# Loading the seventh chunk of modulation weights earlier, and starting VectorE's multiply-and-sums behind the second chunk, in the first stage of a hybrid attention / mLSTM / conv layer on one core

## The chip, the core and the metric

The kernel runs on one core of a Trainium2 chip (trn2). Its engines are TensorE (PE, with its weight load PEld), VectorE (DVE), ScalarE (ACT), GpSimd (POOL) and SyncE (SP, which only issues transfers). The metric is the device time of one execution in microseconds; lower is better.

## The reference

One inference step of a one-layer diffusion backbone over 128 context tokens and 512 latent tokens of width 1024. What the first stage computes is the modulated, normalised input and its first projections:

```
mod = (silu(cond) @ w_ada + b_ada).reshape(B, 6, D)       # cond: c for latent, c_ctx for context tokens
shift1, scale1, gate1, shift2, scale2, gate2 = mod[:, 0..5, None, :]
h = rmsnorm(x, g_pre_mix) * (1 + scale1) + shift1
(na_q, na_k, na_v, m_q, ..., gate_pre) = split(h @ w_in)
```

Everything is float32. The rest of the layer (neighbourhood attention, a bidirectional mLSTM, a short convolution, three gated branches, an output projection, and a SwiGLU feed-forward block) takes the tokens from `h` on.

## The kernel before

All 640 tokens (T) are held at once. The model dimension is cut into eight chunks of 128 (KD = 8). Every large product is made from three float32r matmuls: each operand is split into a high part (a copy to `fp32r` on ACT: `w_hi`, `h_hi`) and a low part (a subtraction on DVE: `w_lo`, `h_lo`), and PE multiplies high by high, high by low and low by high (L2070, L2071, L2072).

A Python function `make_plan` writes one list of steps, and each engine walks the same list and does its part of each step. So the order of the list is the order on every engine, and an engine that waits in one step holds everything behind it. Semaphores are counted.

The first stage runs like this. The tokens are loaded, normalised and turned (steps `xsq`, `xturn`), which gives `xnt`, chunk by chunk, with the channel on the partition. For each chunk k the stage then needs `scale1` and `shift1` of its 128 channels for the two conditions, in `mod`. For chunks 0 to 5 PE makes them: `rows(k)` is an `ada_row` group (16 small matmuls of the chunk's weights `ada0[:, k]` with `cond`, L2117, copied to `adarow` by ACT, L1202), `columns(k)` is an `ada_pair` group (4 matmuls, L2125; DVE adds the bias and the norm weight, L1584 and L1588). For chunks 6 and 7 (`DOT_CHUNKS`) DVE makes them: step `dot k m` is two multiply-and-sums over a row of 1024 (L1744), one for each condition, of half m of `ada0[:, k]` with `condr0`; after the half m = 1 come two small instructions (L1752, L1755). `condr0` holds the two condition rows, the same on all 128 partitions, after a SiLU on ACT (step `dots_in`, L1321). The products themselves go to `prod0s`, which is laid over the token tile `xt`, as is `condr0`.

Step `h k` applies scale and shift to `xnt[:, k]` (DVE for k up to 3, L1766; ACT above, L1332), step `hsplit k` makes `h_hi` (ACT, L1338) and `h_lo` (DVE, L1773), and step `first k` is the part of the first projection (the attention values of all tokens, accumulated in five PSUM banks, 15 matmuls per chunk) that chunk k gives. Called below: unit k. `split_to(n)` makes the high and low part of weight blocks up to n (L1102 and L1476). Block b of weights lies in `raw[:, b % 4]`.

In the list before, `dots_in` stands behind unit 0. `dot 6 0` stands behind `hsplit 3`, `dot 6 1` between `h 4` and `hsplit 4`, `dot 7 0` between `h 5` and `hsplit 5`, and `dot 7 1` between `h 6` and `hsplit 6`.

All loads of the stage but one are issued by SP, in this order: the token tiles and small constants, then `ada0` for chunks 0 to 7, with block 0, 1, 2, 3 of the weights behind chunk 0, 2, 4 and 6, then the other constants, `wm`, the key cache, and the weight blocks from 4 on as their buffers come free. The transfers of one issuing engine are worked off as a queue on the 16 DMA engines. The one exception is `condr0`: GpSimd issues it, when the last token tile is turned (`x_tr`), because it overwrites `xt`.

Of the kernel before, what the change touches and what calls it, by code (L numbers as in the profile page):

```python
# [19 lines left out]
ACT = mybir.ActivationFunctionType  # L20
X = mybir.AxisListType.X

P = 128
D = 1024
KD = D // P
CTX, LAT = 128, 512
T = LAT + CTX
HT = T // 2
TT = T // P
# [77 lines left out]
BLOCKS_HELD = 4  # L107
FIRST_ADA = 8
DOT_CHUNKS = (6, 7)


def parts_of(n):
# [58 lines left out]
def make_plan():  # L171
# [3 lines left out]
    plan, groups = [], []  # L175
# [103 lines left out]
    plan.append(("hsplit", 0))  # L279
    rows(1)  # L280
    columns(1)
    plan += [("h", 1), ("hsplit", 1)]
    dots = [(k, m) for k in DOT_CHUNKS for m in range(2)]
    for k in range(KD):
        c = k + 2
        plan.append(("first", k, 0, 2))
        if c < DOT_CHUNKS[0]:
            rows(c)
        plan.append(("first", k, 2, TT))
        if c < DOT_CHUNKS[0]:  # L290
            columns(c)
        if k % 2 == 0 and c < KD:
            split_to(k // 2 + 2)
        if k == 0:
            plan.append(("dots_in",))
        if c < KD:
            plan.append(("h", c))
            if k in (2, 3, 4):
                plan.append(("dot", *dots.pop(0)))
            plan.append(("hsplit", c))  # L300
            if k == 1:
                plan.append(("dot", *dots.pop(0)))
        if k == 5:
            split_to(5)
        if k == 6:
            group("mif", mif, 0, 0, bank=4)
            group("mif", mif, 0, 1, bank=5)
            split_to(6)
# [76 lines left out]
    m = UNIT_OF[("out", (1,))]  # L385
# [66 lines left out]
    for c in range(2):  # L452
        for i in range(6):
            m = UNIT_OF[("down", (c, i))]
# [114 lines left out]
def program(nc, a, out, vline, gline, xline):  # L569

    ctx = ExitStack()
    with ctx:
# [3 lines left out]
        def at(name, shape, offset, dt=F32):  # L576

            size = 4
            for n in shape[1:]:
                size *= n  # L580
            assert offset + size <= ROOM, name
            return nc.alloc_sbuf_tensor_at(name, shape, dt, offset=base + offset)
# [40 lines left out]
        xnt = at("xnt", [P, KD, T], R1 + 20480)  # L623
        junk = at("junk", [P, D], R1 + 40960 + 2048)
        ada0 = at("ada0", [P, FIRST_ADA, KD * UW], ROOM - FIRST_ADA * KD * UW * 4)
        condr0 = at("condr0", [P, 2, D], R1)
        prod0s = [at(f"dot{c}", [P, D], R1 + 8192 + 4096 * c) for c in range(2)]

        (bo_hi, bo_lo, cl, cout, hsum, mnat, mcols, dec, e_sb, st_sb, kw_sb, tmp_sb, num_sb, merged, gt), _e = chain(
# [42 lines left out]
        def sems(names):  # L672
# [14 lines left out]
        condr0_in, condr0_rd, dot_done, dot_bias, dot_mod = sems(  # L687
            "condr0_in condr0_rd dot_done dot_bias dot_mod")
# [12 lines left out]
        x_sq, x_rstd, x_nrm, x_tr = sems("x_sq x_rstd x_nrm x_tr")  # L701
# [130 lines left out]
        def _(sp):  # L832
            sp.dma_start(cols[:, :], a["cols"]).then_inc(cols_in, 16)
            def load(b):
                if D0 <= b < D0 + BLOCKS_HELD:
                    sp.wait_ge(flo_done, 7 * (WU - 2 + (b - D0) // 2) + 7)
                elif b >= BLOCKS_HELD and is_ada(b - BLOCKS_HELD):
                    sp.wait_ge(ada_done, adas_done(b - BLOCKS_HELD))
                elif b >= BLOCKS_HELD:
                    wait_lo(sp, b - BLOCKS_HELD)  # L840
                sp.dma_start(raw[:, b % BLOCKS_HELD, :], source(b)).then_inc(raw_in[b % BLOCKS_HELD], 16)
# [14 lines left out]
            for t in range(TT):  # L856
                src = a["x_sample"][0, tok(t), :] if t < CH else a["x_prompt"][0]
                sp.dma_start(xt[:, t, :], src).then_inc(x_in[t], 16)
                if t == 0:
                    sp.dma_start(cst[:, 0:160], a["consts"][:, 0:160]).then_inc(const_in, 16)  # L860
            for j in range(KD):
                sp.dma_start(ada0[:, j, :], a["w_first"][j]).then_inc(ada_in[j], 16)
                if j % 2 == 0:
                    load(j // 2)
            sp.dma_start(cst[:, 160:640], a["consts"][:, 160:640]).then_inc(const2_in, 16)
            sp.dma_start(wm[:, :, :], a["w_mif"]).then_inc(wm_in, 16)
            sp.dma_start(kct[:, :, :], a["cache_k"]).then_inc(kc_in, 16)
            for step in PLAN:
# [44 lines left out]
                elif step[0] == "ada_rows":  # L913
# [9 lines left out]
                    src = bass.AP(gline.tensor, q * 2 * D, [[0, P], [D, 2], [1, D]])  # L923
# [39 lines left out]
        def _(pool):  # L963
# [20 lines left out]
            def bias(hp):  # L984
# [6 lines left out]
                for y, free in ((0, 1), (1, 3), (2, 4)):  # L991
# [6 lines left out]
                            braw[:, i, :].rearrange("p (r k) -> p r k", r=ROWS)[:, :, sh:sh + KB],  # L998
                            mask_na[:, y, :].unsqueeze(1).to_broadcast([P, ROWS, KB]), ALU.add)
                    ins.then_inc(bias_rd, 1)  # L1000

            pool.wait_ge(x_tr, 2 * TT)
            src = bass.AP(a["cond_rows"].tensor, 0, [[0, P], [D, 2], [1, D]])
            pool.dma_start(condr0[:, :, :], src).then_inc(condr0_in, 16)
            pool.wait_ge(const2_in, 16)
            for step in PLAN:
                if step[0] == "bias0":
# [40 lines left out]
                elif step[0] == "group" and GROUPS[step[1]]["kind"] == "mo":  # L1048
                    x = GROUPS[step[1]]
                    f, h = x["what"]  # L1050
# [32 lines left out]
        def _(act):  # L1083
# [207 lines left out]
            for step in PLAN:  # L1291
# [26 lines left out]
                    drain(step[1])  # L1318
                elif step[0] == "dots_in":
                    act.wait_ge(condr0_in, 16)  # L1320
                    nc.scalar.activation(condr0[:, :, :], condr0[:, :, :], ACT.Silu).then_inc(condr0_rd, 1)  # L1321
                elif step[0] == "h" and step[1] > 3:
                    k = step[1]
                    act.wait_ge(xt_dve, TT)
# [10 lines left out]
                elif step[0] == "hsplit":  # L1335
                    k = step[1]
                    act.wait_ge(h_aff, k + 1)
                    nc.scalar.activation(h_hi[:, k, :], xnt[:, k, :], ACT.Copy).then_inc(h_hid, 1)  # L1338
                elif step[0] == "na":
                    _, sub, s = step  # L1340
# [122 lines left out]
        def _(dve):  # L1463
# [240 lines left out]
            for step in PLAN:  # L1704
# [30 lines left out]
                elif step[0] == "dot":  # L1735

                    k, m = step[1:]
                    dve.wait_ge(condr0_rd, 1)
                    dve.wait_ge(ada_in[k], 16)
                    n = 2 * DOT_CHUNKS.index(k) + m  # L1740
                    if n:
# [27 lines left out]
                elif step[0] == "hsplit":  # L1769

                    k = step[1]
                    dve.wait_ge(h_hid, k + 1)
                    nc.vector.tensor_tensor(h_lo[:, k, :], xnt[:, k, :], h_hi[:, k, :].bitcast(F32),  # L1773
                                            ALU.subtract).then_inc(h_lod, 1)
                elif step[0] == "na":
# [724 lines left out]
```

## Time and profile before

| | |
|---|---|
| median of 3 runs | 1149.83 us (1148.89 to 1150.03) |
| the profiled execution's own time | 1150.59 us |
| its span | 1148.8 us |
| TensorE busy | 1128.4 us, 98% of the span |
| VectorE busy | 725.4 us, 63% |
| ScalarE busy | 477.5 us, 42% |
| GpSimd busy | 71.2 us, 6% |
| mean granted TensorE clock | 0.997 |

The span runs from the first to the last instruction record of the profiled execution; its own time has 1.8 us more around it. All times below are microseconds from the start of the span. A row of the timeline gives start, duration, engine, line, operation, output and input, and in brackets how long the engine was idle before and what released it. Durations of back-to-back matmuls overlap; the pace is the distance of their starts.

### The profile page before, as it was taken

The numbers are of one execution on the slowest core, as the hardware profiler recorded it, in microseconds if no ns is written. First come the engines' busy times: TensorE is split into PE (matmuls) and PEld (weight loads), VectorE is DVE, ScalarE is ACT, GpSimd is POOL, SyncE is SP. The second block draws the span as 40 slices with busy tenths as digits, with TensorE's granted clock in tenths as the row PEclk, the third lists the DMA queues.
The fourth block names the chain that finished last, engine by engine and source line by source line (L and its number), as shares of the span: only waits on it lengthen the run. The fifth ranks groups of instructions, "written<-read, shape, count | busy, mean of one in ns | idle before, by whom it ended". The sixth has DMA issues, their size and how long they took to land.

```text
span 1148.8 us, 18558 instructions
## 1 busy us (share of the span) xinstructions
PE 1128.4 (98%) x7358; PEld 1061.3 (92%) x7358; DVE 725.4 (63%) x1290; ACT 477.5 (42%) x881; POOL 71.2 (6%) x123
## 2 busy tenths in 40 slices
PE   5999999999999999999999999999999999999997
PEld 4699999889999999999999988999999999988886
DVE  4724545449675666588795446899997777633444
ACT  4544443443334334322222337655555555533431
POOL 2032111000000000220000002100000000000002
PEclk9999999999999999999999999999999999999999
DMA  9666121132431121336654244234322232315112
GB/s 364 231 194 146 56 75 56 37 92 74 76 73 55 56 74 56 111 128 185 202 177 136 68 137 155 81 130 146 129 83 102 75 119 103 110 56 196 61 37 92
DMA packets 40150, 130.22 MB, mean 113 GB/s; under 512 B 8736, under 2 KB 10304, under 8 KB 38528
## 3 DMA queue, kind: packets, MB, share of 16 engines
q1 hardware_dynamic: 36592, 121.41, 32.6%
q0 software_dynamic: 3472, 7.62, 2.3%
q8 instruction: 59, 0.97, 0.4%
q14 instruction: 27, 0.22, 0.1%
HBM read 121.64 MB, written 7.36 MB: 112 GB/s over the span
## 4 chain that ended last, share of the span: by engine, by line
PE 92%; DVE 5%; ACT 1%; issue 1%; DMA 1%; SPq 0%; POOL 0%; POOLq 0%; ACTq 0%; DVEq 0%
PE ps L2070 28%; PE ps L2072 28%; PE ps L2071 28%; PE ps L2275 1%; PE ps L2314 1%; PE ps L2298 1%; PE ps L2366 1%; PE ps L2368 1%; PE ps L2370 1%; DMA xt<-in_x_sample 1%; PE ps L2242 1%; PE ps L2352 0%; PE ps L2117 0%; DVE w_lo L1476 0%; DVE dot L1744 0%
## 5 line engine op out<-in xcount | busy, mean ns | idle before, releaser
L2072 PE MATMUL ps<-h_hi,w_lo 128*128 128x320 f32 x1184 | 365.9, 309 | 0.0
L2070 PE MATMUL ps<-h_hi,w_hi 128*128 128x320 f32 x1024 | 322.6, 315 | 0.2 <-DVE w_hi L1601 0.2
L2071 PE MATMUL ps<-h_lo,w_hi 128*128 128x320 f32 x1024 | 316.3, 309 | 0.0
L2072 PEld LDWEIGHTS ps<-h_hi,w_lo 128*128 128x128 f32 x1184 | 222.3, 188 | 0.0
L1476 DVE TENSOR_TENSOR w_lo<-raw,w_hi 128x1024 fp32r<-128x1024 f32 x109 | 132.7, 1227 | 111.7 <-ACT w_hi L1102 111.2
L2070 PEld LDWEIGHTS ps<-h_hi,w_hi 128*128 128x128 f32 x1024 | 192.6, 188 | 2.4 <-DVE w_hi L1601 0.5
L2071 PEld LDWEIGHTS ps<-h_lo,w_hi 128*128 128x128 f32 x1024 | 192.5, 188 | 0.1
L2070 PE MATMUL ps<-w_hi,h_hi 128*128 128x512 f32 x380 | 151.0, 397 | 1.2 <-DVE h_lo L1773 1.1
L2072 PE MATMUL ps<-w_hi,h_lo 128*128 128x512 f32 x380 | 148.6, 391 | 0.0
L2071 PE MATMUL ps<-w_lo,h_hi 128*128 128x512 f32 x380 | 148.4, 391 | 0.0
L1102 ACT ACTIVATE w_hi<-raw 128x1024 fp32r<-128x1024 f32 x109 | 113.3, 1052 | 32.9 <-PE ps L2072 32.3
L2070 PEld LDWEIGHTS ps<-w_hi,h_hi 128*128 128x128 f32 x380 | 71.6, 188 | 18.8 <-issue 4.0
L2072 PEld LDWEIGHTS ps<-w_hi,h_lo 128*128 128x128 f32 x380 | 71.6, 188 | 15.3
L2071 PEld LDWEIGHTS ps<-w_lo,h_hi 128*128 128x128 f32 x380 | 71.7, 189 | 14.1
L1193 ACT ACTIVATE gt<-ps,half_bg 128x320 f32<-128x320 f32 x48 | 25.4, 529 | 137.7 <-PE ps L2072 137.7
L2070 PE MATMUL ps<-h_hi,w_lo 128*128 128x320 f32 x240 | 74.4, 310 | 0.8 <-ACT snap L1240 0.8
L2071 PE MATMUL ps<-h_lo,w_lo 128*128 128x320 f32 x240 | 74.2, 309 | 0.0
L2070 PE MATMUL ps<-tt_hi,w_hi 128*128 128x320 f32 x240 | 73.9, 308 | 0.0
L2071 PE MATMUL ps<-tt_lo,w_hi 128*128 128x320 f32 x240 | 73.9, 308 | 0.0
L2072 PE MATMUL ps<-tt_hi,w_hi 128*128 128x320 f32 x240 | 73.9, 308 | 0.0
L1522 DVE TENSOR_TENSOR h_lo<-ff,h_hi 128x1280 fp32r<-128x1280 f32 (+1 forms) x22 | 30.5, 1429 | 64.4 <-ACT h_hi L1130 64.4
L1489 DVE SCALAR_TENSOR_TENSOR prod<-raw,condr 128x1024 f32<-128x1024 f32 x48 | 57.1, 1227 | 14.1 <-ACT condr L1314 12.9
(275 smaller groups left out, 1836.3 us busy)
## 6 DMA issues: line engine op xcount, KB each, us to landing
raw<-in_w_blocks SPq DMA_DIRECT2D x182, 512.0 KB, 3.8
ada<-in_w_first SPq DMA_DIRECT2D x8, 1024.0 KB, 19.4
xline<-x SPq DMA_DIRECT2D x5, 512.0 KB, 5.3
x<-xline SPq DMA_DIRECT2D x5, 512.0 KB, 8.0
xt<-in_x_sample SPq DMA_DIRECT2D x4, 512.0 KB, 6.7
condr<-in_cond_rows POOLq DMA_DIRECT2D x2, 1024.0 KB, 7.0
vtok<-vline POOLq DMA_DIRECT2D x8, 256.0 KB, 10.4
g<-gline SPq DMA_DIRECT2D x2, 1024.0 KB, 6.9
```

What stands on the lines that cost most here:

```text
L1102: ins = nc.scalar.activation(held(w_hi, b), raw[:, s, :], ACT.Copy)
L1193: nc.scalar.activation(gt[:, f, half(h)], bank, ACT.Tanh, scale=0.5, bias=half_bg[:, t:t + 1]).then_inc(act_drain, 1)
L1476: nc.vector.tensor_tensor(held(w_lo, b), raw[:, s, :], held(w_hi, b).bitcast(F32), ALU.subtract).then_inc(lo_done, 1)
L1489: ins = nc.vector.scalar_tensor_tensor(prod[c][:, :], raw[:, b % BLOCKS_HELD, :], 1.0, condr[:, c, :], ALU.mult, ALU.mult, accum_out=to)
L1522: nc.vector.tensor_tensor(h_lo[:, o2 + k:o2 + k + n, :], ff[:, k0 + k:k0 + k + n, :], h_hi[:, o2 + k:o2 + k + n, :].bitcast(F32), ALU.subt ...
L2070: nc.tensor.matmul(dst, wh, xh, start=first, stop=False, skip_group_check=resumed)
L2071: nc.tensor.matmul(dst, wh, xl, start=False, stop=False, skip_group_check=resumed)
L2072: return nc.tensor.matmul(dst, wl, xh, start=False, stop=last, skip_group_check=resumed)
L2242: ins = nc.tensor.transpose(turned_x(t, hh)[:, kk, :], xt[:, t, tok(4 * hh + kk)], ident)
L2275: ins = nc.tensor.matmul(dst[:, NKEY:512], src, pt[:, n % 2, i, c * P:(c + 1) * P], start=(c == 0), stop=(c == 2))
L2298: nc.tensor.matmul(A[i][:, 0:256], q, kk, start=True, stop=True)
L2314: ins = nc.tensor.transpose(A[2 + i][:, c * P:(c + 1) * P], sx[:, n % 2, i, c * P:(c + 1) * P], ident)
```

## The change

Four things are changed.

1. SP loads the first-stage weights in the order 0, 1, 2, 6, 3, 4, 5, 7 (`FIRST_ORDER`). The weight blocks 0 to 3 go behind the first, third, fifth and seventh of these, as before.
2. `condr0` is loaded by SP, behind the third chunk and block 1, and no longer by GpSimd. It now lies in the place of `h_hi` and `h_lo` of chunks 6 and 7 (one condition in each), so it needs no wait for the token tiles. `hsplit 6` and `hsplit 7` wait on ACT and on DVE for all four `dot` steps (`dot_done`). The `dot` steps wait for the turned tokens (`x_tr`), since the products still go over `xt`.
3. `dots_in` and `dot 6 0` stand behind `hsplit 1`, before unit 0.
4. `dot 6 1` stands behind `hsplit 2`, `dot 7 0` behind `hsplit 3`, and `dot 7 1` between `h 5` and `hsplit 5`. None is left between `h 4` and `hsplit 4`, nor between `h 6` and `hsplit 6`.

```diff
+FIRST_ORDER = (0, 1, 2, 6, 3, 4, 5, 7)
...
-    plan += [("h", 1), ("hsplit", 1)]
-    dots = [(k, m) for k in DOT_CHUNKS for m in range(2)]
+    plan += [("h", 1), ("hsplit", 1), ("dots_in",), ("dot", DOT_CHUNKS[0], 0)]
+    dots = [(k, m) for k in DOT_CHUNKS for m in range(2)][1:]
...
-        if k == 0:
-            plan.append(("dots_in",))
         if c < KD:
             plan.append(("h", c))
-            if k in (2, 3, 4):
+            if k == 3:
                 plan.append(("dot", *dots.pop(0)))
             plan.append(("hsplit", c))
-            if k == 1:
+            if k < 2:
                 plan.append(("dot", *dots.pop(0)))
...
-        condr0 = at("condr0", [P, 2, D], R1)
+        condr0 = at("condr0", [P, 2, KD * T], 3 * BLOCKS_HELD * 4096 + DOT_CHUNKS[0] * T * 4)[:, :, 0:D]
...
-            for j in range(KD):
+            for i, j in enumerate(FIRST_ORDER):
                 sp.dma_start(ada0[:, j, :], a["w_first"][j]).then_inc(ada_in[j], 16)
-                if j % 2 == 0:
-                    load(j // 2)
+                if i % 2 == 0:
+                    load(i // 2)
+                if i == 2:
+                    src = bass.AP(a["cond_rows"].tensor, 0, [[0, P], [D, 2], [1, D]])
+                    sp.dma_start(condr0, src).then_inc(condr0_in, 16)
...
-            pool.wait_ge(x_tr, 2 * TT)
-            src = bass.AP(a["cond_rows"].tensor, 0, [[0, P], [D, 2], [1, D]])
-            pool.dma_start(condr0[:, :, :], src).then_inc(condr0_in, 16)
...
                     k = step[1]
                     act.wait_ge(h_aff, k + 1)
+                    if k >= DOT_CHUNKS[0]:
+                        act.wait_ge(dot_done, 2 * len(DOT_CHUNKS))
                     nc.scalar.activation(h_hi[:, k, :], xnt[:, k, :], ACT.Copy).then_inc(h_hid, 1)
...
                     dve.wait_ge(condr0_rd, 1)
+                    dve.wait_ge(x_tr, 2 * TT)
                     dve.wait_ge(ada_in[k], 16)
...
                     dve.wait_ge(h_hid, k + 1)
+                    if k >= DOT_CHUNKS[0]:
+                        dve.wait_ge(dot_done, 2 * len(DOT_CHUNKS))
```

## Rows read from the trace of the kernel before

**Rows 1.** The page: busy time, share of the span and instructions of each engine.
```profile
PE 1128.4 (98%) x7358; PEld 1061.3 (92%) x7358; DVE 725.4 (63%) x1290; ACT 477.5 (42%) x881; POOL 71.2 (6%) x123
```

**Rows 2.** The chain of waits, 44 to 54 us: start, duration, what.
```profile
49.49 2.39 DVE dot L1744 x4
...
52.26 0.75 DVE h_lo L1773
...
53.14 0.47 PE ps L2070
```

**Rows 3.** TensorE's timeline: first matmul of units 4 and 5, last of unit 5.
```profile
44.94 0.47 PE L2070 MATMUL ps<-w_hi,h_hi 128*128 128x512 f32 x1
...
48.42 0.47 PE L2070 MATMUL ps<-w_hi,h_hi 128*128 128x512 f32 x1
...
51.70 0.39 PE L2072 MATMUL ps<-w_hi,h_lo 128*128 128x512 f32 x1
```

**Rows 4.** VectorE's timeline, 25 to 46 us, in its order.
```profile
25.20 0.82 DVE L1773 TENSOR_TENSOR h_lo<-xnt,h_hi 128x640 fp32r<-128x640 f32 x1 [0.81 <-ACT h_hi L1338]
...
29.77 0.16 DVE L1588 SCALAR_TENSOR_TENSOR mod<-mod,cols 128x2 f32<-128x2 f32 x1
...
32.59 0.82 DVE L1773 TENSOR_TENSOR h_lo<-xnt,h_hi 128x640 fp32r<-128x640 f32 x1 [0.81 <-ACT h_hi L1338]
34.68 0.16 DVE L1584 TENSOR_TENSOR mod<-ps,cols 128x4 f32<-128x4 f32 x1 [1.27 <-PE ps L2125]
...
36.85 0.82 DVE L1773 TENSOR_TENSOR h_lo<-xnt,h_hi 128x640 fp32r<-128x640 f32 x1 [0.80 <-ACT h_hi L1338]
37.59 1.22 DVE L1744 SCALAR_TENSOR_TENSOR dot<-ada,condr 128x1024 f32<-128x1024 f32 x1
...
40.08 0.16 DVE L1588 SCALAR_TENSOR_TENSOR mod<-mod,cols 128x2 f32<-128x2 f32 x1
...
41.29 1.22 DVE L1744 SCALAR_TENSOR_TENSOR dot<-ada,condr 128x1024 f32<-128x1024 f32 x1
...
43.97 0.82 DVE L1773 TENSOR_TENSOR h_lo<-xnt,h_hi 128x640 fp32r<-128x640 f32 x1
44.91 0.16 DVE L1584 TENSOR_TENSOR mod<-ps,cols 128x4 f32<-128x4 f32 x1
...
45.22 1.23 DVE L1744 SCALAR_TENSOR_TENSOR dot<-ada,condr 128x1024 f32<-128x1024 f32 x1
```

**Rows 5.** ScalarE's timeline, 24 to 42 us, in its order.
```profile
24.43 0.74 ACT L1338 ACTIVATE h_hi<-xnt 128x640 fp32r<-128x640 f32 x1 [2.37 <-DVE xnt L1766]
...
29.18 1.92 ACT L1321 ACTIVATE condr<-condr 128x2048 f32<-128x2048 f32 x1 [0.85 <-DMA condr<-in_cond_rows]
...
40.35 1.20 ACT L1332 ACTIVATE xnt<-xnt,mod 128x512 f32<-128x512 f32 x2 [1.80 <-DVE mod L1588]
41.59 0.74 ACT L1338 ACTIVATE h_hi<-xnt 128x640 fp32r<-128x640 f32 x1
```

**Rows 6.** SyncE's issues of weight block 1 and of chunk 7.
```profile
7.28 0.58 SPq L841 DMA_DIRECT2D raw<-in_w_blocks  x1
...
14.82 2.14 SPq L862 DMA_DIRECT2D ada<-in_w_first  x1
```

**Rows 7.** Transfers alone, same two issues: count, size, us from issue to landing.
```profile
raw<-in_w_blocks SPq DMA_DIRECT2D x1, 512.0 KB, 15.0
...
ada<-in_w_first SPq DMA_DIRECT2D x1, 1024.0 KB, 26.1
```

**Rows 8.** Transfers in the windows 0 to 20.4 us and 0 to 38.1 us.
```profile
DMA packets 1733, 6.95 MB, mean 341 GB/s; under 512 B 212, under 2 KB 468, under 8 KB 1338
...
DMA packets 2956, 14.33 MB, mean 376 GB/s; under 512 B 350, under 2 KB 664, under 8 KB 1816
```

**Rows 9.** The page, DMA issues: later loads of a condition-like row pair, by each queue.
```profile
condr<-in_cond_rows POOLq DMA_DIRECT2D x2, 1024.0 KB, 7.0
...
g<-gline SPq DMA_DIRECT2D x2, 1024.0 KB, 6.9
```

**Rows 10.** Windows: us, busy of PE, PEld, DVE, ACT, POOL, then granted clock, DMA.
```profile
20.40:26.00 5.60, 3.75 (x14) 2.69 (x18) 4.42 (x9) 1.88 (x4) 0.00 (x0) 0.70 1.02 424
51.93:57.00 5.07, 4.01 (x20) 2.89 (x23) 3.08 (x5) 2.89 (x4) 0.00 (x0) 1.00 0.10 42
```

More of the change, by code:

```diff
@@ L1320, in _ @@
                     act.wait_ge(condr0_in, 16)
-                    nc.scalar.activation(condr0[:, :, :], condr0[:, :, :], ACT.Silu).then_inc(condr0_rd, 1)
+                    nc.scalar.activation(condr0, condr0, ACT.Silu).then_inc(condr0_rd, 1)
                 elif step[0] == "h" and step[1] > 3:
```

## The prediction

> **What bounds the kernel now.** I read the page's engine table first: PE is busy 98% of the span [rows 1], so a change on DVE and in the loads can only give back what PE idles. Then the chain of waits, in the stage that the change touches: from 23 us on it runs from matmul to matmul, except at one place, where it goes through the four instructions of `dot 7 1`, then `h_lo` of chunk 6, then the first matmul of unit 6 at 53.14 [rows 2]. Third, PE's timeline around it: the last matmul of unit 5 starts at 51.70, and at the pace of this stage (15 matmuls from 48.42 on, so (51.70 - 48.42) / 14 = 0.23) the next could start at 51.93 [rows 3]. It starts at 53.14 [rows 2]. So 1.21 us is all that there is to win here. The cause is in DVE's order: a half of a dot with its two small instructions takes 43.97 - 41.29 = 2.68 [rows 4], and one of them stands right before the `h_lo` that PE wants next. Last I read SP's issues and landings, since the change reorders the loads: they decide what follows.
>
> **The loads.** This is where I expect the gain to go. Up to 38.1 us the DMA engines had moved 14.33 MB [rows 8]. That is what the queue holds through chunk 7: tokens and constants 2.77 MB, eight chunks of 1.05 MB, four blocks of 0.52 MB, and `condr0`, 1.05 MB, together 14.3 MB. `condr0` came over GpSimd's queue in the middle of that, so it is in this sum before and after. Between 20.4 and 38.1 us 7.38 MB moved, 0.417 MB/us, with no gap. So moving `condr0` to SP and chunk 6 ahead doesn't change the moment at which the last byte of chunk 7 has been moved: about 38.1 us. Its landing before was 14.82 + 26.1 = 40.9 [rows 6, 7], 2.8 us behind the volume. Block 1, before `condr0` was in flight, landed at 7.28 + 15.0 = 22.3 [rows 6, 7], where the volume through it, 6.97 MB, was moved at 20.4 [rows 8]: 1.9 us behind. With `condr0` in the same queue the lag could stay 1.9 (landing 40.0) or be 2.8 again (40.9). I take the middle, 40.5, and call it t7. Before, nobody wanted chunk 7 until 45.22 [rows 4].
>
> What the row shows is a lag of 1.9 ahead of the transfer over GpSimd's queue and 2.8 behind it [rows 6 to 8]. The Trainium skill, "DMA: Bandwidth & Descriptors", section "Latency and other measured facts", has as its best guess that some of the 16 DMA engines are slowed by the descriptor rings of GpSimd's queue, which the SP queue doesn't have. By that rule the lag stays 1.9 and t7 is 40.0; the trace agrees in direction, but doesn't show the cause.
>
> The other landings: `condr0` is done by volume at 20.4 + 1.05 / 0.417 = 22.9, lands 24.8 to 25.7; chunk 6 lands 27.3 to 28.2, I take 27.8; chunk 3, 2.5 later, 29.8 to 30.7, just ahead of its `rows` at 31.0. Chunks 4 and 5 and block 2 are over 1.5 us ahead of their use. SP itself issues later by what the queue holds back, but its next loads stand behind 1 MB more in the same queue and are used only from 54 us on: nothing. GpSimd loses a wait and an issue at 19.7 and has nothing behind them until 64 us: nothing.
>
> **The steps, in the order of the list.**
>
> *`dots_in` behind `hsplit 1`.* On ACT `h_hi` of chunk 1 ends at 24.43 + 0.74 = 25.17, and the SiLU takes 1.92 [rows 5]. It runs 25.2 to 27.1, or up to 27.6 if `condr0` lands late. ACT's next work, a copy at 27.00, loses 0.1 to 0.6, which PE, busy with unit 0 until 29.0, hides. Cost 0.
>
> *`dot 6 0`.* DVE is idle after `h_lo` of chunk 1 (25.20 + 0.82) until it takes up the columns of chunk 2, whose second instruction is at 29.77 [rows 4]. The dot starts when chunk 6 lands, 27.8. From a dot without the small instructions to the second column instruction it is 40.08 - 37.59 = 2.49 [rows 4]: 30.29, so chunk 2 is 0.5 later, from 0 with a landing at 27.3 to 0.9 at 28.2. Its `h_lo` then starts at 33.1 instead of 32.59 and ends before unit 2 begins (34.5). Cost 0; the cover left is 0.4.
>
> *`dot 6 1` behind `hsplit 2`.* It starts 37.59 - 36.85 = 0.74 behind the `h_lo`, at 33.85, and the columns of chunk 3 come 2.68 later, at 36.53 instead of 34.68. `h_lo` of chunk 3 moves from 36.85 to 38.70 and ends at 39.52 [rows 4]; unit 3 begins at 39.7. Cost 0 to 0.4 (chunk 6 late), and that is taken up by the next stall.
>
> *`dot 7 0` behind `hsplit 3`.* DVE is ready for it at 39.4, but its operand lands at t7 = 40.5. Here an unneeded transfer becomes a wait, and behind it on DVE, in order, stand the columns of chunk 4, the low half of block 2 and `h_lo` of chunk 4; ACT's `h 4` and `h_hi`, and behind them its copy for the rows of chunk 5, hang on them, and so does PE. Step by step from t7: 2.49 to the second column instruction, 40.35 - 40.08 = 0.27 to `h 4`, 41.59 - 40.35 = 1.24 to `h_hi`, 25.20 - 24.43 = 0.77 to `h_lo`, 0.82 for it, and 53.14 - 53.01 = 0.13 to PE [rows 2, 4, 5]. Sum 5.72: unit 4 starts at 46.22, not 44.94 [rows 3]. Loss 1.28.
>
> *`dot 7 1` between `h 5` and `hsplit 5`.* From the `h_lo` of chunk 4 (t7 + 4.77): 0.74 to the columns of chunk 5, 45.22 - 44.91 = 0.31 to the dot, 2.68 to `h_lo` (before it was 2.3, without the small instructions), 0.82 and 0.13 [rows 2, 4]: unit 5 starts at t7 + 9.45 = 49.95. Unit 4 lasts 48.42 - 44.94 = 3.48 [rows 3], until 49.70. Loss 0.25.
>
> *No dot before `hsplit 6`.* ACT's `h_hi` of chunk 6 comes at about 50.6, the `h_lo` ends by 52.2, the new waits for `dot_done` are met at 48.9, and unit 5 lasts until 49.95 + 3.51 = 53.46. The stall of 1.21 is gone.
>
> Sum: 1.28 + 0.25 - 1.21 = +0.32 us; unit 6 starts at 53.46 instead of 53.14. From there on both lists are the same and PE is fed well ahead, so I take it as handed on to the end undiminished. The profiled execution would take 1150.59 + 0.32 = 1150.9; it lay 0.76 above the median of the runs, so the median goes from 1149.83 to 1150.2. The sum moves one for one with t7: at 40.0 it is -0.2, at 40.9 +0.7, and it is zero at 40.2.
>
> **The rivals.**
>
> *A: chunk 7 lands in time.* If it lands by 39.4, DVE never waits. Then `h_lo` of chunk 5 alone is late (dot at 45.22, + 2.68 + 0.82 + 0.13 = 48.85, against 48.42), and unit 6 starts at 52.36: -0.8, time 1149.0. For it: the lag ahead of `condr0` was short. Against it: it needs a lag of 1.3, and the smallest that the rows show is 1.9.
>
> *B: the clock falls in the new stall.* PE would idle over 1 us in one piece ahead of the columns of chunk 5, at 44.5. In the trace a pause from 20.4 to 22.2 was followed by a stretch at the lower level: over 20.4 to 26.0 the granted clock is 0.70, which is 1.7 us lost (5.6 x 0.30); the pause of 1.21 before unit 6 was followed by full clock [rows 10]. If the new one does as the first: +0.3 + 1.7, time 1151.8; with t7 at 41.2 or later it passes +2.3. Against it: PE was busy without a break for 20 us before. The Trainium skill, "TensorE: Matmul & The Clock Gate", section "Part 1: The HAM clock gate", says that the low level (1.2 GHz) is the default and sustained activity gives the full one; by it a pause like this can, but need not, cost a stretch at half pace, as in B.
>
> *C: slower than before, because the replicated load is dear on SP's queue.* `condr0` is one row pair read for 128 partitions, now in pieces of 4 KB. Later loads of the same form took 6.9 us from issue to landing on SP's queue and 7.0 on GpSimd's, with others in flight [rows 9]. If it held the queue for all of 6.9 less the lag of 1.9, 5.0 instead of 2.5, everything behind it would be 2.5 later: t7 = 43.0, sum +2.8, time 1152.6. It decides from t7 = 40.2 on. Against it: both kinds of queue show the same time, and over GpSimd's the rate of the whole stayed 0.417.
>
> *D: the seventh chunk isn't there either,* so that the early dots only shift the wait: at a landing over 28.7 unit 2 and 3 stall as well; but all of this is swallowed by the wait for chunk 7, time 1150.4. I count it with the forecast.
>
> **How the numbers follow.** Forecast with D (t7 from 39.9 to 41.2): 0.70. A: 0.13. B: 0.09. C: 0.08. The likeliest gives 1150.2. To either side the range goes to A's end and B's, and adds that medians of three runs differ by some tenths: 1148.8 to 1152.0. A measurement of this kernel can tell about 0.2% (2.3 us) from no change: only C, and B with a late t7, lie beyond, 0.08; faster by that much isn't open to a stall of 1.21, 0.02 for what I haven't seen; the rest, 0.90, is within.
>
> **What would show it.** Right: a wait of DVE before L1744 at about 39.4 for the load of chunk 7, the columns of chunk 4 after 42.7, PE idle over 1 us between the rows and the columns of chunk 5, unit 4 starting near 46.2, none before unit 6, unit 6 near 53.5. Wrong: the third pair of dots starting straight behind `h_lo` of chunk 3 (A), a clock below 1 after 44.5 (B), chunk 6 landing after 30 (C), or a difference of the whole that isn't there at unit 6.

## The result, and the profile after

| | before | after |
|---|---|---|
| median of 19 runs each | 1150.49 us | 1152.29 us (1151.31 to 1155.15) |
| ratio, with its 95% interval | 1 | 1.0017 (1.0010 to 1.0024) |
| profiled execution, own time | 1150.59 | 1151.69 |
| its span, mean granted clock | 1148.8, 0.997 | 1149.9, 0.996 |

The change makes the kernel slower, by 0.1 to 0.24%. The median lies 2.1 us above the predicted 1150.2 and just outside the range.

The same kernel was run twice more beside others: 1.0014 (1.0005 to 1.0023) and 1.0009 (1.0000 to 1.0018). Over all its 43 runs its mean is 1152.38 +- 0.32. Over the 114 runs of the kernel before that stood beside the later ones (four repeat the numbers of another and are counted once) it is 1151.04 +- 0.25: a difference of 1.34 us where +0.32 was predicted. Each run gives its span and its mean granted clock, so a time can be split in two: (1 - clock) x span, which the lowered clock took, and the rest. Before: 3.96 and 1147.08 +- 0.18. After: 4.58 +- 0.34 and 1147.80 +- 0.26. So about 0.72 +- 0.3 us of the 1.34 is work or waiting that came on top, and 0.6 +- 0.4 goes with the clock. (The clock is given to three digits, 1.15 us a step, so that the split is good for means of many runs only.) This split is used again below.

The page's engine row answers to [rows 1]:

```profile
PE 1130.0 (98%) x7358; PEld 1062.8 (92%) x7358; DVE 725.5 (63%) x1290; ACT 477.1 (41%) x881; POOL 70.4 (6%) x122
```

PE's timeline after, the place of [rows 3]: the first matmuls of units 0, 3, 4, 5 and 6, and the columns of chunk 5.

```profile
21.82 0.76 PE L2073 MATMUL ps<-w_hi,h_hi 128*128 128x512 f32 x1
...
38.49 0.50 PE L2073 MATMUL ps<-w_hi,h_hi 128*128 128x512 f32 x1
...
45.21 0.58 PE L2128 MATMUL ps<-cst,adarow 128*128 128x2 f32 x4 [1.78 <-ACT adarow L1200]
45.80 0.47 PE L2073 MATMUL ps<-w_hi,h_hi 128*128 128x512 f32 x1
...
49.76 0.50 PE L2073 MATMUL ps<-w_hi,h_hi 128*128 128x512 f32 x1 [0.29 <-DVE h_lo L1776]
...
53.29 0.39 PE L2073 MATMUL ps<-w_hi,h_hi 128*128 128x512 f32 x1
```

The pause has moved as predicted. There is none before unit 6 (it starts 3.53 after unit 5), and there is one of 1.78 before the columns of chunk 5. The row names ACT's copy as what ended it, and that is only the last link. The chain of waits shows the first one:

```profile
17.80 22.07 DMA ada<-in_w_first
...
40.06 2.38 DVE dot L1745 x4
...
42.82 1.21 ACT xnt L1330 x2
...
44.05 0.74 ACT h_hi L1338
44.79 0.28 ACT adarow L1200
...
45.21 0.59 PE ps L2128 x4
```

The chain reaches a transfer: chunk 7, issued at 17.80, landed 22.07 later, at 39.87. VectorE's timeline, the place of [rows 4], has the wait for it behind `h_lo` of chunk 3 (the earlier row is `dot 6 0`):

```profile
26.70 1.23 DVE L1745 SCALAR_TENSOR_TENSOR dot<-ada,condr 128x1024 f32<-128x1024 f32 x1 [1.92 <-DMA ada<-in_w_first]
...
37.60 0.83 DVE L1776 TENSOR_TENSOR h_lo<-xnt,h_hi 128x640 fp32r<-128x640 f32 x1 [0.81 <-ACT h_hi L1338]
...
40.06 1.23 DVE L1745 SCALAR_TENSOR_TENSOR dot<-ada,condr 128x1024 f32<-128x1024 f32 x1 [1.62 <-DMA ada<-in_w_first]
...
44.82 0.83 DVE L1776 TENSOR_TENSOR h_lo<-xnt,h_hi 128x640 fp32r<-128x640 f32 x1 [0.98 <-ACT h_hi L1338]
45.82 0.16 DVE L1584 TENSOR_TENSOR mod<-ps,cols 128x4 f32<-128x4 f32 x1 [0.17 <-PE ps L2128]
...
46.20 1.23 DVE L1745 SCALAR_TENSOR_TENSOR dot<-ada,condr 128x1024 f32<-128x1024 f32 x1
```

One thing differs from the forecast at sight: unit 3 starts at 38.49, not at 39.62, and all of PE's front is 1.1 to 1.2 us earlier than in the trace of before (unit 0 at 21.82, not 23.03). Yet unit 6 is no earlier: 53.29 against 53.14 [rows 2].

### The profile page after: what moved, and what is told of

Its sections match the earlier page's. It is cut to its first block, busy times and chain, and to the rows that moved or that the text cites. A ratio compares the mean times of both kernels' runs of the same rounds, so it can differ in the third digit from the quotient of the medians.

```text
span 1149.9 us, 18565 instructions
## 1 busy us (share of the span) xinstructions
PE 1130.0 (98%) x7358; PEld 1062.8 (92%) x7358; DVE 725.5 (63%) x1290; ACT 477.1 (41%) x881; POOL 70.4 (6%) x122
## 4 chain that ended last, share of the span: by engine, by line
PE 93%; DVE 2%; DMA 2%; SPq 1%; ACT 1%; issue 0%; POOLq 0%; POOL 0%; DVEq 0%; ACTq 0%
PE ps L2073 29%; PE ps L2074 28%; PE ps L2075 28%; DMA ada<-in_w_first 2%; PE ps L2278 1%; PE ps L2317 1%; PE ps L2301 1%; PE ps L2369 1%; SPq L861 1%; PE ps L2371 1%; PE ps L2373 1%; PE ps L2355 0%; DVE dot L1745 0%; PE ps L2357 0%; SPq L840 0%
```

## The experiments

All ratios are to the kernel before, run in the same session. "Unit 6 - unit 0" is the distance from the first matmul of unit 0 to that of unit 6 in the run's trace; before it was 53.14 - 23.03 = 30.11, after 53.29 - 21.82 = 31.47. Most traces have a stretch at the lower clock inside this distance, which makes it some 1.3 us longer; e4 and e11 have none. What each was expected to do stands as it was written before it ran.

### The two kernels again, and the wait taken away

**e1, e2: the kernel before and the changed kernel again**, no edit.

> The kernel before, unchanged, as a control. Every theory: ratio 1.000, interval across 1. By the theory of the landing (T1), the start of unit 0 moves by up to 1.2 us from execution to execution with the landing of the second token tile, and unit 6 moves with it one for one, 30.1 us behind unit 0. By the rival of the clock (T3) the granted clock is 1.00 from 27 us to the last few us.

> The changed kernel, unchanged, a second look. All theories: 1.0017 again, +1.1 to +2.8 us. T1 (DVE waits for the landing of chunk 7 behind hsplit 3): DVE's third pair of dots begins at 40.0 to 40.9 after a wait for the load, PE is idle 1.2 to 1.9 us ahead of the columns of chunk 5, unit 6 starts 12.9 to 13.3 us behind that dot, wherever unit 0 stood. T3 (stretches at the lower clock make most of the loss): a dip near 45 or near 277 us again; if there is none here and the time is still over +1 us, T3 isn't the main cause.

Measured: 1.0000 (0.9991 to 1.0009), and 1.0014 (1.0005 to 1.0023). So the slowdown is real. In e2 unit 0 starts at 22.01 and `dot 7 0` at 39.75; in e1 unit 0 starts at 21.09 and unit 3 at 36.41. Both kernels' heads vary by more than the effect that is looked for. VectorE's timeline of e2:

```profile
39.75 1.23 DVE L1745 SCALAR_TENSOR_TENSOR dot<-ada,condr 128x1024 f32<-128x1024 f32 x1 [1.58 <-DMA ada<-in_w_first]
```

**e3: all four dots read chunk 6**, so that none waits for chunk 7; the modulation of chunk 7 is left out of the output.

```diff
-                    dve.wait_ge(ada_in[k], 16)
+                    dve.wait_ge(ada_in[DOT_CHUNKS[0]], 16)
...
-  ... ada0[:, k, m * D:(m + 1) * D] ...
+  ... ada0[:, DOT_CHUNKS[0], m * D:(m + 1) * D] ...
```

> The changed kernel, but all four dots read chunk 6 and wait for chunk 6 alone; left out: chunk 7's own modulation (its two dots use chunk 6's weights). All loads and the order of steps stay. T1: the wait ahead of the third pair is gone, the pair starts behind hsplit 3 at 37 to 39, unit 6 starts 29.3 to 29.5 behind unit 0 (before 30.1), the time is 0.6 to 0.9 us under before (ratio 0.9992 to 0.9998). T2 (the reordered loads or the replicated load on SP's queue are dear in themselves): it stays +1 to +2 us. T3: stays +1 or more, with dips of the clock.

Measured: 0.9999 (0.9987 to 1.0011), unit 6 - unit 0 = 29.69. In VectorE's timeline of e3 the third pair has no wait in brackets:

```profile
40.35 1.22 DVE L1745 SCALAR_TENSOR_TENSOR dot<-ada,condr 128x1024 f32<-128x1024 f32 x1
```

With the same loads, list and instructions, the slowdown is gone once the wait on chunk 7's landing is: the mean is 1150.91 +- 1.03, and the part without the clock 1147.18 +- 0.39, 0.6 +- 0.5 below the changed kernel. From unit 3 to unit 6 it takes 12.81, before 13.52. The runs carry this, not the trace: its front is a late one (unit 0 at 24.17, unit 3 at 41.05), which would hardly have waited anyway.

**e4: chunk 7 loaded ahead of chunk 5 and of block 3.**

```diff
-FIRST_ORDER = (0, 1, 2, 6, 3, 4, 5, 7)
+FIRST_ORDER = (0, 1, 2, 6, 3, 4, 7, 5)
...
-                if i % 2 == 0:
-                    load(i // 2)
+                if i % 2 == 0 and i < 6 or i == 7:
+                    load(3 if i == 7 else i // 2)
```

> The changed kernel with chunk 7 loaded ahead of chunk 5, and weight block 3 behind chunk 5 (order 0, 1, 2, 6, 3, 4, 7, 5). Same bytes, same dots. T1: chunk 7 lands at 36 to 37, chunk 5 at 38.5 to 39.5, ahead of its rows at 40 to 41; no wait ahead of the third pair; 0.5 to 0.9 us under before, as with the dots on chunk 6. T2: still slower than before by 1 to 2 us, since the same transfers run in the same queue. T3: no dip at 45, the one at 277 unchanged, so between the two.

Measured: 0.9992 (0.9981 to 1.0004), mean 1150.40 +- 0.88: beside the changed kernel the loss is gone, beside the kernel before a gain isn't shown. The trace has the cure and a second late landing. VectorE's timeline, then PE's, of e4:

```profile
38.21 1.22 DVE L1745 SCALAR_TENSOR_TENSOR dot<-ada,condr 128x1024 f32<-128x1024 f32 x1
```

```profile
30.11 1.07 PE L2120 MATMUL ps<-ada,cond 128*32 128x256 f32 x16 [1.73 <-DMA ada<-in_w_first]
```

`dot 7 0` waits for nothing, though unit 3 starts early in this trace, at 38.76; unit 6 follows 12.76 behind it. But the rows of chunk 3, which the new load order sets behind chunk 6 and `condr0`, make PE wait 1.73 us.

### Loads alone, the queue, and a later head

**e5: only the loads of the change**, with the dots where the kernel before has them.

```diff
-    plan += [("h", 1), ("hsplit", 1), ("dots_in",), ("dot", DOT_CHUNKS[0], 0)]
+    plan += [("h", 1), ("hsplit", 1)]
...
+        if k == 0:
+            plan.append(("dots_in",))
...
-            if k == 3:
+            if k in (2, 3, 4):
...
-            if k < 2:
+            if k == 1:
```

> The new loads, the new place of the condition rows and the new waits, with the order of steps of the kernel before (dots_in behind unit 0, dots at their old places). T1: nothing of the loss is here: ratio 1.000 (within 0.3 us), unit 6 starts 30.1 us behind unit 0 with the stall of 1.2 before it. T2 (the loads are dear): the loss of 1 to 2 us is here. T3: no statement but that the clock is as in before.

Measured: 1.0007 (0.9997 to 1.0018), mean 1152.03 +- 0.76, unit 6 - unit 0 = 33.23. I had expected nothing of the loss here, within 0.3 us of before; the mean is 1.0 +- 0.8 above it. PE's timeline of e5 has two new waits:

```profile
30.09 1.94 PE L2122 MATMUL ps<-ada,cond 128*32 128x256 f32 x16 [2.29 <-DMA ada<-in_w_first]
...
54.28 0.47 PE L2075 MATMUL ps<-w_hi,h_hi 128*128 128x512 f32 x1 [1.54 <-DVE h_lo L1778]
```

The first is chunk 3 again. The second I had missed: `hsplit 6` now waits on ACT for all four dots, and in this list `dot 7 1` comes right before it, so that ACT's `h_hi` can't run beside the dot as it did. ACT's timeline of e5:

```profile
52.54 0.74 ACT L1340 ACTIVATE h_hi<-xnt 128x640 fp32r<-128x640 f32 x1 [2.56 <-DVE dot L1747]
```

Unit 5 to unit 6 takes 5.24 in it, 4.72 before: 0.5 us for the shared place of `condr0`, in the old list only.

**e6: `condr0` over GpSimd's queue**, all else as in the change.

```diff
-                if i == 2:
-                    sp.dma_start(condr0, src).then_inc(condr0_in, 16)
...
+            pool.dma_start(condr0, src).then_inc(condr0_in, 16)
             pool.wait_ge(const2_in, 16)
```

> The changed kernel, but the condition rows are loaded over GpSimd's queue, issued when its small work is done (about 16 us), to their new place. It tells whether the lag of chunk 7's landing behind the volume comes from the other queue. If the transfer over GpSimd's queue makes the lag: chunk 7 lands at 40.7 to 41.3 instead of 40.0 to 40.4, and the kernel is 0.5 to 1 us slower than the changed one. If not: the same time as the changed kernel within 0.4 us. T2 in its form 'the replicated load is dear on SP's queue': 0.5 us or more faster than the changed kernel.

Measured: 1.0015 (1.0007 to 1.0023), the same as the changed kernel. VectorE's timeline of e6:

```profile
40.46 1.23 DVE L1744 SCALAR_TENSOR_TENSOR dot<-ada,condr 128x1024 f32<-128x1024 f32 x1 [0.95 <-DMA ada<-in_w_first]
```

With `condr0` on SP's queue chunk 7's dot started at 40.06, 39.75, 40.11 and, in the one later trace that waited, at 41.52 (e16). 40.46 lies inside (it landed at 40.27, where 40.0 to 40.4 or 40.7 to 41.3 had been expected for the two cases). So that the load is dear on SP's queue (rival C) isn't supported, and whether GpSimd's queue lengthens the lag stays open.

**e7, e8: two more 512-wide instructions of VectorE ahead of the second token tile**, in the kernel before and in the changed one: PE's front should start later, the loads don't.

```diff
+        spare = at("spare", [P, 512], 82432)
...
                     dve.wait_ge(x_rstd, t + 1)
+                    if t == 1:
+                        dve.wait_ge(x_nrm, 1)
+                        for _ in range(2):
+                            link(nc.vector.tensor_tensor(spare[:, :], xt[:, 0, 0:512], xt[:, 0, 512:D], ALU.mult))
```

> The kernel before with two added multiplications on DVE (128x512, about 1.3 us together) ahead of the second token tile's normalisation: the head comes later by 0.9 to 1.3 us. T1: before, PE is bound from unit 0 on, so the time grows by that, +0.9 to +1.3 us. The rival (the first stage of before is tied to the loads too): +0.3 or less.

> The changed kernel with the same two added multiplications. T1: the wait for chunk 7's landing swallows the later head: it takes the same time as the changed kernel within 0.4 us, although unit 0 starts 0.9 to 1.3 us later, and the distance from the kernel before with the later head is 0.3 to 1.0 us instead of about 2. Rival (the loss is a fixed piece of work or waiting added behind unit 0, T2 or T3): it grows by 0.9 to 1.3 us, as before does.

Measured: 1.0016 (1.0006 to 1.0026) and 1.0016 (1.0005 to 1.0026); means 1152.87 +- 0.72 and 1153.05 +- 0.80. The late head costs the kernel before 1.8 us and the changed one 0.7. What the change adds shrinks from 1.34 to 0.2 +- 1.1. In the trace of e8 unit 3 starts at 41.55 and `dot 7 0` waits for nothing (VectorE's timeline of e8):

```profile
40.85 1.22 DVE L1750 SCALAR_TENSOR_TENSOR dot<-ada,condr 128x1024 f32<-128x1024 f32 x1
```

Unit 6 - unit 0 is 29.59 in it, against 30.19 in e7. Unit 0 starts at 24.72 in e8, but at 23.36 in e7, no later than in the kernel before at times (23.34 and 23.55 in e15 and e13). The means alone don't exclude the old difference, so these two runs are no proof by themselves; with the traces they fit that the change loses where PE's front is early, and not where it is late.

### One dot moved, and chunk 3 ahead

**e9, e12: the kernel before with `dot 7 1` behind `hsplit 6`**, loads untouched.

```diff
-            if k in (2, 3, 4):
+            if k in (2, 3):
...
-            if k == 1:
+            if k in (1, 4):
```

> The kernel before with one step moved: dot 7 1 stands behind hsplit 6 instead of between h 6 and hsplit 6 (only unit 7 needs it). Loads, condition rows and all else as before. If the stall ahead of unit 6 is all that was to be won: it goes, for early and late heads alike, unit 6 starts 28.8 to 29.1 behind unit 0 (before 30.1) in an execution with the same clock, the mif product waits 0 to 0.5 us for h 7, and the time is 0.7 to 1.3 us under before (ratio 0.9989 to 0.9994). If the stall is only handed on (to h 7, which then comes behind the dot): same as before within 0.3 us, with PE waiting ahead of the mif product or of unit 7.

> e9 again, to halve its interval and to see a second head: same numbers as e9.

Measured: 0.9997 (0.9988 to 1.0006) and 0.9996 (0.9987 to 1.0004). Unit 6 - unit 0 is 28.89 and 29.16, so the stall of 1.21 is gone without a new one. Timelines of PE and VectorE in e9:

```profile
22.11 0.76 PE L2070 MATMUL ps<-w_hi,h_hi 128*128 128x512 f32 x1
...
50.77 0.39 PE L2072 MATMUL ps<-w_hi,h_lo 128*128 128x512 f32 x1
51.00 0.39 PE L2070 MATMUL ps<-w_hi,h_hi 128*128 128x512 f32 x1
...
54.49 2.36 PE L2133 MATMUL ps<-xnt,wm 128*32 128x320 f32 x32
```

```profile
49.28 0.82 DVE L1773 TENSOR_TENSOR h_lo<-xnt,h_hi 128x640 fp32r<-128x640 f32 x1 [0.63 <-ACT h_hi L1338]
50.03 1.22 DVE L1744 SCALAR_TENSOR_TENSOR dot<-ada,condr 128x1024 f32<-128x1024 f32 x1
```

Unit 6 follows unit 5 at the pace of 0.23. Over the 22 runs of both, the part without the clock is 1145.94 +- 0.31, 1.14 below before, what the stall was worth. The clock's part is 4.54, 0.58 more than before, and the mean (1150.48 +- 0.41) only 0.56 +- 0.48 lower, where 0.7 to 1.3 had been expected. Neither interval of the ratio excludes no change, so this isn't shown to beat the kernel before; it does beat the change.

**e10: as e5, with the chunks loaded in their order and `condr0` behind chunk 3.**

```diff
-FIRST_ORDER = (0, 1, 2, 6, 3, 4, 5, 7)
+FIRST_ORDER = (0, 1, 2, 3, 4, 5, 6, 7)
...
-                if i == 2:
+                if i == 3:
```

> As e5 (the order of steps of before, condition rows on SP's queue in their new place), but the chunks are loaded in the order of before and the condition rows behind chunk 3. If e5's loss is PE's wait for chunk 3, pushed back by the condition rows and chunk 6 in executions with an early head: no wait of the rows matmuls (L2117 in before) for a load, time within 0.4 us of before. If the loss comes from the replicated load on SP's queue or from the new place of the condition rows: +0.5 to +1.5 us as in e5.

Measured: 1.0007 (0.9999 to 1.0016), mean 1151.57 +- 0.62. The rows of chunk 3 don't wait (PE's timeline of e10). That agrees with the wait being the load order's, but the front of this trace is late (unit 0 at 23.13, in e5 at 21.05), so it isn't shown by it alone:

```profile
31.16 1.07 PE L2122 MATMUL ps<-ada,cond 128*32 128x256 f32 x16
```

Unit 5 to unit 6 takes 5.23, as in e5: the wait of `hsplit 6` once more.

**e11: the changed kernel a third time.**

> The changed kernel unchanged, third look, for the spread of its head. T1: unit 6 again 13.2 us behind the third pair of dots, that pair at the landing of chunk 7 (39.7 to 40.9) or behind hsplit 3 if unit 3 starts later than 40; with an early head also a wait of the rows of chunk 3 for their load. Ratio 1.001 to 1.002. Rival (a fixed loss): unit 6 the same distance behind unit 0 as in the other two looks (31.0 to 31.5).

Measured: 1.0009 (1.0000 to 1.0018). It shows both late landings in one trace, PE's timeline and then VectorE's:

```profile
30.00 1.07 PE L2120 MATMUL ps<-ada,cond 128*32 128x256 f32 x16 [1.02 <-DMA ada<-in_w_first]
```

```profile
40.11 1.23 DVE L1745 SCALAR_TENSOR_TENSOR dot<-ada,condr 128x1024 f32<-128x1024 f32 x1 [1.24 <-DMA ada<-in_w_first]
```

### The clock's part

Windows over 275 to 283 us, of before and then of after (the columns of [rows 10]; 1.00 is the full level, 2.4 GHz, and 0.79 a mix of it with the low one, 1.2 GHz):

```profile
275.00:283.00 8.00, 7.74 (x58) 7.49 (x57) 6.38 (x17) 1.13 (x5) 0.00 (x0) 1.00 0.45 132
```

```profile
275.00:283.00 8.00, 8.00 (x51) 7.98 (x51) 5.69 (x15) 0.05 (x1) 0.00 (x0) 0.79 0.42 131
```

**e13 to e16: filling matmuls** in the stretch of short instructions that comes ahead of that place, in the kernel before (e13, e15) and in the changed one (e14, e16), to keep the clock up in both and compare them without it.

```diff
+                    def filler():
+                        nc.tensor.matmul(A[3][:, 0:512], h_hi[:, 0, 0:P], h_hi[:, 0, 0:512], start=True, stop=True)
                     for c in range(TT):
+                        filler()
+                        filler()
...
+                            filler()
```

The last stands before each of the 8 pairs of small products behind that loop. The fillers write a bank that another step uses, so PE also waits for that step first (`+ pe.wait_ge(na_out, len(NA_UNITS))`); the trace of e13 shows no idle time of PE there.

> The kernel before with 18 added matmuls (128x512, about 0.22 us each at full clock, into an unused bank) among the short transposes and matmuls of step mcols. They add 3 to 4 us. If the stretch at the lower clock at 275 to 284 us comes from that run of short instructions, no trace shows it any more, and the run-to-run scatter falls. If it doesn't, the stretch stays.

> The changed kernel with the same 18 matmuls. T1 alone: 0.7 to 1.3 us slower than e13 and e15 in the mean, with the same mean granted clock. Rival (the change itself costs clock, by its pauses in the first stage): 1.4 us or more slower than e13 and e15, with a mean granted clock lower by 0.0004 or more, and stretches at the lower clock at 44 to 50 us in the trace.

> As e13, to halve the interval: the same time within 0.5 us, and no stretch at the lower clock at 275 to 284 us if the short instructions are its cause.

> As e14, to halve the interval: 0.7 to 1.3 us slower than e13 and e15 if only the stage's waits count, 1.4 us or more if the change costs clock as well.

Measured: 1.0086 (1.0071 to 1.0101), 1.0097 (1.0083 to 1.0111), 1.0088 (1.0074 to 1.0102), 1.0096 (1.0082 to 1.0110). They miss their aim: the fillers cost 10.3 us in the kernel before and 10.1 in the changed one (means 1161.35 and 1162.44), where 3 to 4 had been expected, and the low stretch didn't go, it came later and lasted twice as long, in both. (e8, which has no fillers, has a stretch as long, at 277 to 285.) Window of e13, then of e14:

```profile
283.00:290.00 7.00, 7.00 (x23) 5.66 (x23) 0.19 (x1) 0.00 (x0) 0.00 (x0) 0.51 0.00 0
```

```profile
283.00:290.00 7.00, 7.00 (x25) 6.26 (x25) 0.19 (x1) 0.00 (x0) 0.00 (x0) 0.54 0.00 0
```

Between the two pairs the change adds 1162.44 - 1161.35 = 1.09 +- 0.86 us, which tells neither 0.7 from 1.3 nor what the clock adds. The traces give one more landing-bound case and one that isn't: e14 (unit 3 at 40.65, no wait, unit 6 - unit 0 = 29.66) and e16 (30.95), whose VectorE's timeline has:

```profile
41.52 1.23 DVE L1745 SCALAR_TENSOR_TENSOR dot<-ada,condr 128x1024 f32<-128x1024 f32 x1 [1.45 <-DMA ada<-in_w_first]
```

## Why the prediction was right or wrong, point by point

**Right: what bounds the stage, and where the stall goes.** The stall before unit 6 was worth 4.72 - 3.53 = 1.19 (1.21 predicted), and it went. The wait for chunk 7 took its place, with everything on DVE, ACT and PE that was named as queued behind it. e3 and e4 show this wait as the cause of the part that isn't the clock's. Of the five traces of the changed list with an unaltered head (after, e2, e11, and e14 and e16, whose fillers lie far behind) four wait for chunk 7; rival A holds in the fifth, e14; C isn't supported (e6).

**Right: the steps behind the landing.** From `dot 7 0` to unit 4 it takes 45.80 - 40.06 = 5.74 (5.72 predicted), 5.74 in e2 as well. The dot starts 0.19 behind the landing at 39.87, for which I had allowed nothing.

**Missed by under 1 us: the landing, t7.** It was taken as 40.5, between 40.0 and 40.9. By the chains of waits chunk 7 landed at 39.87, 39.56 and 39.92 in after, e2 and e11, all three just below the lower bound, and at 41.33 in e16, above the upper one. An earlier landing makes the loss smaller: with the dot at 40.06 and nothing else changed, the prediction's sum would be -0.12. So this isn't what made the prediction too low.

**Small miss: unit 5 at t7 + 9.45.** It is 49.76 - 40.06 = 9.70. I ran the columns of chunk 5 from VectorE's side alone. They came at 45.82 and not t7 + 5.51 = 45.57, since PE's column matmuls waited for ACT's copy, which stands behind `h_hi` of chunk 4. So unit 6 is 13.23 to 13.25 behind the dot in all five landing-bound traces (after, e2, e6, e11, e16), 12.96 predicted: +0.28.

**Wrong, and the step that decided: "unit 4 starts at 46.22, not 44.94 [rows 3]. Loss 1.28".** The landing hangs on the load stream, and 44.94 on PE's front; I took the front of a single execution, and it was a late one. The traces reduce to two rules: before, unit 6 = unit 3 + 13.5 (also in e7, e13 and e15, but not in e1, see below); after, unit 6 = the later of unit 3 + 12.8 and `dot 7 0` + 13.24. So the change wins 0.7 if unit 3 starts late. It comes out even when unit 3 is 0.26 ahead of the dot, and each tenth more than that costs a tenth. With unit 3 at 39.62 the dot at 40.06 would have cost 0.2. With its own 38.49 it cost 53.30 - 51.99 = 1.3. The terms, in its own trace and against before's distances between units:

| term | predicted | in the trace after |
|---|---|---|
| unit 4 late | +1.28 | 45.80 - (38.49 + 5.32) = +1.99 |
| unit 5 late | +0.25 | 3.96 - 3.48 = +0.48 |
| stall before unit 6 | -1.21 | -1.19 |
| sum | +0.32 | +1.28 |

In the runs without a change to the head, unit 0 started anywhere from 21.1 to 24.2, from 21.1 to 22.2 in about half of them. Over the same five traces (after, e2, e11, e14, e16) the two rules give +1.3, +0.9, +0.9, -0.7 and +0.5 us, a mean of +0.6, beside the 0.72 +- 0.3 that its runs show apart from the clock. e7 and e8 are the direct test, but a weak one: with the head made late the change costs 0.2 +- 1.1.

The kernel before hangs on a landing too, once its front is early enough, and its trace of e1 shows it. Chunk 6 landed at 36.07, and `dot 6 0` waited for it. VectorE's timeline of e1, then PE's:

```profile
36.16 1.22 DVE L1744 SCALAR_TENSOR_TENSOR dot<-ada,condr 128x1024 f32<-128x1024 f32 x1 [1.70 <-DMA ada<-in_w_first]
```

```profile
43.51 0.74 PE L2070 MATMUL ps<-w_hi,h_hi 128*128 128x512 f32 x1 [1.62 <-DVE h_lo L1773]
```

Unit 4 starts 43.51 - 36.16 = 7.35 behind that dot, as it does in the trace of before (44.94 - 37.59), and 1.8 later than unit 3 + 5.32. So before can't start unit 6 ahead of about 36.16 + 7.35 + 8.20 = 51.7 (an estimate, with 8.20 from unit 4 to unit 6 in the trace of before), after not ahead of 40.06 + 13.24 = 53.3: by these two traces the change costs about 1.6 at most, however early the front.

**Wrong in the same way: chunk 3, "just ahead of its `rows` at 31.0".** It landed as forecast (29.97 in e4, 29.95 in e5, in 29.8 to 30.7), but with an early front PE waits 0.3 to 2.3 us for it (e4, e5, e6, e11), and e10, whose front was late, has no such wait. In the changed kernel the wait for chunk 7 swallows most of it, as rival D had it; in e4 it eats the gain. In e11 unit 3 itself is late by this wait, so that the +0.9 above, taken at the same unit 3, leaves it out; against the 51.7 of before it is 1.6.

**Too low by the baseline.** 1150.2 stood on a median of 3 runs, 1149.83; over 19 runs it is 1150.49. Of the 2.1 us between forecast and measured median 0.66 is this. The rest is the change: +1.8 between the medians, or +1.34 between the means of all runs, where +0.32 had been forecast. (A slip in rival B changes nothing: by the prediction's own sum it passes +2.3 from t7 = 40.8 on, not 41.2.)

**Half right: the clock (B).** The new pause itself brought no drop, in this trace or in the other landing-bound ones: over the 2.6 us from 43.4 the granted clock was 1.00.

```profile
43.40:46.00 2.60, 0.81 (x6) 0.76 (x6) 1.43 (x3) 1.63 (x4) 0.00 (x0) 1.00 0.44 113
```

But the other 0.6 us of the mean goes with the clock, and where I said that the difference is "handed on to the end undiminished" it grew. In the two first traces the kernels stand level behind the stage (the matmuls behind it begin at 63.42 and 63.45), and the 1.1 us of their spans arises at 275 to 283: 0.79 against 1.00, 8 x 0.21 = 1.7 us. (From 1140 us on some comes back: 0.86 against 0.76 in before.) That stretch at half pace is in all other kept traces (with the fillers some us later), e1 (the kernel before again) with them, and is absent only in the first trace of before and in e7. The profiled execution of before was a lucky one in this. Whether the change makes the stretch more frequent, or 43 runs drew it more often, stays open; e9 and e12, with another order of the dots and the old loads, have as large a clock's part (4.54). So the cause of nearly half of the 1.34 isn't shown.

## What to carry to other kernels

The cover between an engine's front and a landing is the difference of two times that vary apart from each other. Take both from several executions, of the kernel before as well, and ask what the step costs at the early end of the front and the late end of the load, not at the one trace. Where the consumer of a load is moved ahead on an in-order engine, everything behind it waits for that landing; moving the work later, behind what PE wants next, removed the same stall without needing any load (e9, e12). And where a shared buffer needs a new wait, follow that wait on every engine that takes it, in every order of the list in which it will stand: it cost nothing in the new list and 0.5 us in the old one (e5, e10).

## What the runs showed of the hardware that was not expected

- The start of unit 0 moved by up to 3 us between the 16 traces without a change to the head (21.1 to 24.2), and by 1.9 between two traces of the kernel before (23.03, and 21.09 in e1). In e1 unit 3 started at 36.41, where before had 39.62. Of these 3.2 us 1.3 is the stretch at half pace, which mostly begins between 21 and 25 us, ahead of unit 3, and here fell at 43 to 47. Window of e1:

```profile
43.00:47.00 4.00, 3.49 (x8) 2.81 (x9) 3.96 (x9) 3.22 (x5) 0.00 (x0) 0.57 0.12 44
```

- A pause of 1.8 us of PE was followed by a low clock at 20.4 to 22.2 in before [rows 10], and by none at 43.4 to 45.2 in after. The Trainium skill, "TensorE: Matmul & The Clock Gate", section "Part 1: The HAM clock gate", has the high level follow from sustained activity. What PE did just before the pause doesn't tell the two cases apart: in e1 a pause of 1.62, behind over 20 us of dense matmuls, was followed by the stretch above (0.57 over 43 to 47), and in e1, e4 and e11 the pause of 1.6 to 1.8 ahead of unit 0 was followed by no low stretch. No run here varied it alone.
- 512-column matmuls put between short instructions didn't hold the clock up: the low stretch came about 6 us later and twice as long as in after (clock 0.51 and 0.54 over 283 to 290). A stretch as long stands in e8 without them, so the length isn't shown to be their doing.
